# Scores of two heads from the two halves of the rows, weights scaled on GpSimd, and a new order, in a 512-token network kernel on one core

## The reference

```python
# first block, compressed/selected/window attention: 8 heads in 2 groups of 4, width 64, causal blocks of 128
ps = masked_softmax(jnp.einsum('bghqd,bgqmd->bghqm', qb, ksel) * scale, smask)
pw = masked_softmax(jnp.einsum('bghqd,bgkd->bghqk', qb, kwin) * scale, wmask)
on = gates[..., 0:1] * o_cmp + gates[..., 1:2] * o_slc + gates[..., 2:3] * o_win
# second block, even layer (differential attention, 4 heads, two softmax maps each)
sc = jnp.einsum('bqhmd,bshmd->bhmqs', qb, k).astype(f32) * scale
p = jax.nn.softmax(sc, axis=-1)
w = (p[:, :, 0] - lam * p[:, :, 1]).astype(v.dtype)
# second block, odd layer: 8 heads of width 96 (latent attention), then 8 heads in 2 groups, width 64
out_c = gqa_attention(q[:, :, :, None, :], k, v_c).reshape(b, s, MLA_HEADS * MLA_V)
out_d = gqa_attention(qd, kd, vd).reshape(b, s, GQA_Q_HEADS * GQA_DIM)
```

## Time and profile before

| | |
|---|---|
| median of 3 runs | 3011.55 us (3011.3 to 3012.63) |
| the profiled execution | 3006.02 us, of which the span from first to last instruction 3004.2 us |
| busy in the span | PE 2838.3 us (94%), PE weight loads 2327.3 (77%), DVE 1662.4 (55%), ACT 1139.8 (38%), POOL 205.2 (7%) |
| granted TensorE clock, mean | 0.976 of full |
| read from HBM | 238.31 MB, 80 GB/s over the span |

### The profile page before, as it was taken

The page is one execution under the profiler, slowest core; times in us unless marked ns, Lnnn a source line. Parts: engine busy times, 40 slices in busy tenths (PEclk is TensorE's granted clock), DMA queues, the critical chain, the costliest instruction groups (busy, mean ns, idle before and its releaser), DMA issues.

```text
span 3004.2 us, 33494 instructions
## 1 busy us (share of the span) xinstructions
PE 2838.3 (94%) x13102; PEld 2327.3 (77%) x13102; DVE 1662.4 (55%) x2501; ACT 1139.8 (38%) x1768; POOL 205.2 (7%) x194
## 2 busy tenths in 40 slices
PE   6997998999999999999799999999999887899999
PEld 5776776888878888877578888888887666688887
DVE  6467665555465443547854444544445987644433
ACT  4454563322233222344633222422233766432322
POOL 1001332000000000002100000000000321000000
PEclk9998999999999999999799999999999999999999
DMA  3212103332323333231023332333321110133322
GB/s 128 77 57 64 58 29 107 104 104 92 99 84 99 98 99 98 90 94 49 8 85 98 97 94 89 100 98 99 98 84 52 33 36 22 42 94 96 99 94 82
DMA packets 71181, 242.58 MB, mean 81 GB/s; under 512 B 8016, under 2 KB 9936, under 8 KB 70768
## 3 DMA queue, kind: packets, MB, share of 16 engines
q1 hardware_dynamic: 68112, 230.85, 24.5%
q0 software_dynamic: 1760, 7.49, 0.7%
q10 hardware_dynamic: 1152, 2.10, 0.2%
HBM read 238.31 MB, written 2.10 MB: 80 GB/s over the span
## 4 chain that ended last, share of the span: by engine, by line
PE 84%; DVE 11%; issue 2%; ACT 2%; POOL 0%; DMA 0%; DVEq 0%; ACTq 0%; POOLq 0%
PE ps L302 83%; DVE SC L325 3%; DVE SM L331 1%; PE ps L305 1%; DVE PTL L313 1%; DVE SC L313 1%; DVE WL L313 1%; DVE SC L319 1%; ACT SC L310 0%; DVE SC L328 0%; DVE NQ L313 0%; DVE SM L339 0%; DVE GQ L313 0%; POOL SC L313 0%; DMA PR<-par 0%
## 5 line engine op out<-in xcount | busy, mean ns | idle before, releaser
L302 PE MATMUL ps<-HH,WH 128*128 128x512 f32 (+1 forms) x2192 | 863.9, 394 | 15.2 <-DVE HL L325 13.6
L302 PE MATMUL ps<-HL,WH 128*128 128x512 f32 (+1 forms) x2192 | 856.4, 391 | 0.0
L302 PE MATMUL ps<-HH,WL 128*128 128x512 f32 (+1 forms) x2192 | 856.3, 391 | 0.0
L313 DVE TENSOR_TENSOR WL<-WF,WH 128x1024 fp32r<-128x1024 f32 (+3 forms) x473 | 546.6, 1161 | 355.8 <-ACT WH L310 353.0
L310 ACT ACTIVATE WH<-WF 128x1024 fp32r<-128x1024 f32 (+3 forms) x473 | 467.0, 993 | 645.3 <-PE ps L302 645.2
L302 PEld LDWEIGHTS ps<-HH,WH 128*128 128x128 f32 (+1 forms) x2192 | 413.5, 189 | 102.6 <-issue 15.3
L302 PEld LDWEIGHTS ps<-HH,WL 128*128 128x128 f32 (+1 forms) x2192 | 412.8, 188 | 88.3
L302 PEld LDWEIGHTS ps<-HL,WH 128*128 128x128 f32 (+1 forms) x2192 | 413.3, 189 | 84.3
L302 PE MATMUL ps<-AH,WH 128*128 128x512 f32 x880 | 342.7, 389 | 3.9 <-DVE AL L313 3.9
L302 PE MATMUL ps<-AH,WL 128*128 128x512 f32 x880 | 342.3, 389 | 0.0
L302 PE MATMUL ps<-AL,WH 128*128 128x512 f32 x880 | 342.3, 389 | 0.0
(11 more groups left out here) (292 smaller groups left out, 3081.2 us busy)
## 6 DMA issues: line engine op xcount, KB each, us to landing
WF<-wall SPq DMA_DIRECT2D x397, 512.0 KB, 3.5
WF<-wall SPq DMA_DIRECT2D x40, 384.0 KB, 2.9
WF<-wall SPq DMA_DIRECT2D x17, 256.0 KB, 2.6
X<-xT ACTq DMA_DIRECT2D x8, 256.0 KB, 11.8
X<-xT POOLq DMA_DIRECT2D x8, 256.0 KB, 2.9
outT<-X POOLq DMA_DIRECT2D x8, 256.0 KB, 2.3
WF<-wall SPq DMA_DIRECT2D x4, 288.0 KB, 3.0
LT<-late POOLq DMA_DIRECT2D x1, 1152.0 KB, 5.5
```

The lines of the kernel that those rows point to most:

```text
L302: return self.real.matmul(o, l, r, start=start, stop=stop, skip_group_check=True)
L313: return self.real.tensor_tensor(o, a, b, op) if self.real is not None else Uncounted()
```

## The change

**What it does.** (1) In N and G the two heads i and i+4, which use the two key groups, are scored together; in D the two softmax maps of a head. Query tiles now hold the high parts of both heads on their two halves of rows, a second tile the low parts, and the keys likewise. A pair takes six matmuls of 64 rows instead of four of 128, dealt out in turn to rows 0 to 63 and 64 to 127 and into two banks. (2) So a query or key tile pair is filled by one ACT copy and one POOL subtraction of 128x512 (`unstacked` holds everywhere but in Q), and no DVE work. (3) In D, L and G the scaling of the weights goes from DVE to POOL as a two-scalar `tensor_scalar`; in D the second scalar is lambda, which removes a small DVE product, and a new step `joined` holds the final subtraction. (4) N and G get a second set of `PT` tiles, so that a pair's two heads don't share one, and N a second product bank. (5) Arena places and the waits that guard them change, and with them the order tables of M, N, D, L and G. (6) `c_made` and `s_product` issue the same matmuls with the halves in alternation.

The tables (a line of each; the rest alters likewise) and the core of the diff:

```diff
-GATES_IN = {"M": (0, 23), "N": (0, 85)}
+GATES_IN = {"M": (0, 23), "N": (0, 72)}
 D_PLACE = {
-    "made": (0.265, -0.033), "largest": (0.768, 0), "raised": (1.266, 0.3), "normed": (2.206, 0.126),
+    "made": (0, 0.049), "largest": (0.863, -0.196), "raised": (1.686, -0.016), "normed": (2.107, 0),
+    "joined": (2.705, 0.048), "turned": (3.631, -0.082), "high": (3.752, 0.15), "low": (4.402, 0.011),
...
+def attend_pair(ph, pair, T, *ends):
+
+    core = ("largest", "raised", "normed", "turned", "high", "low")
+    steps = [("made", 0, (pair, T))]
+    for g, job in enumerate(heads_of(ph, pair)):
+        steps += [(s, g, (job, T)) for s in core] + ([(s, g, job) for s in ends[g]] if T == 3 else [])
+    return steps
...
     items = []
     for i in range(4):
-        for g in range(2):
-            a = [attend((i, g), T, PAIR + (("parts",) if g else ())) for T in range(4)]
-            items += a[:1] + ([rope(f"gq{i + 1}")] if g == 0 and i < 3 else []) + a[1:] + [[]]
+        for T in range(4):
+            items += [attend_pair("G", i, T, PAIR, PAIR + ("parts",)), []]
+            if T == 0 and i < 3:
+                items.append(rope(f"gq{i + 1}"))
+        items.append([])
     return in_turn(G_PLACE, *items)
...
+                if stage == "made" and ph in "NG":
+                    pair, T = key
+                    n, tk = 128 * (T + 1) if causal else S, slice(128 * T, 128 * T + 128)
+                    q, k, made = qk_of(ph, pair)
+                    heads = [(job, T) for job in heads_of(ph, pair)]
+                    for w in made + [w for head in heads for w in bank_left(ph, "s", head)]:
+                        e.wait_ge(*w)
+                    for i in range(3):
+                        for g, head in enumerate(heads):
+                            l, r = three([part[rows(g), tk] for part in q], [part[rows(g), 0:n] for part in k])[i]
+                            done = e.matmul(bank(ph, "s", head)[:, 0:n], l, r, i == 0, i == 2 and not causal)
...
                 elif stage == "made":
                     job, T = key
                     tk = slice(128 * T, 128 * T + 128)
-                    for w in q_made("D", f"eq{job}") + [pooled["D", "lo1", f"ek{job}"]]:
-                        e.wait_ge(*w)
+                    Q, K = EQ[job % 2], EK[job % 2]
+                    e.wait_ge(*pooled["D", "lo1", f"eq{job}"])
+                    e.wait_ge(*pooled["D", "lo1", f"ek{job}"])
                     for m in range(2):
-                        Q, K, p = EQ[job % 2][m], EK[job % 2][m], bank("D", f"s{m}", key)
                         for w in bank_left("D", f"s{m}", key):
                             e.wait_ge(*w)
-                        for i in range(2):
-                            done = e.matmul(p[:, :], Q[:, i, tk], K[:, :], i == 0, i == 1)
-                        done.then_inc(*scored("D", f"made{m}", key))
+                    for i in range(3):
+                        for m in range(2):
+                            l, r = three((Q[0][rows(m), tk], Q[1][rows(m), tk]), (K[0][rows(m), :], K[1][rows(m), :]))[i]
+                            done = e.matmul(bank("D", f"s{m}", key), l, r, i == 0, i == 2)
...
-                    if ph == "L" and key[0] == "m":
-                        e.activation(pair_of(ph, key)[0][:, :], y[0:96, :], ACT.Copy).then_inc(*split_high(ph, "hi1", key))
+                    if unstacked(ph, key):
+                        high, n = pair_of(ph, key)[0], rope_of(ph, key)[0]
+                        e.activation(high[:, :], y[0:n, :], ACT.Copy).then_inc(*split_high(ph, "hi1", key))
...
             for stage, key in order["D"]:
-                rope_stage("D", stage, key)
+                if stage == "normed":
+                    P, sm = tile("D", "P1", key), small("D", "m1", key)
+                    e.wait_ge(*stepped["D", "inverse1", key])
+                    e.wait_ge(*stepped["E", "lam"])
+                    e.wait_ge(*pooled.so_far())
+                    e.tensor_scalar(P, P, sm[:, 2:3], LM[:, 5:6], ALU.mult, ALU.mult).then_inc(*pooled("D", "normed", key))
+                else:
+                    rope_stage("D", stage, key)
...
+            for ph in "LG":
+                for stage, key in order[ph]:
+                    if stage == "normed":
+                        P, sm = tile(ph, "P", key), small(ph, "m", key)
+                        e.wait_ge(*stepped[ph, "normed", key])
+                        e.wait_ge(*pooled.so_far())
+                        e.tensor_scalar(P, P, sm[:, 2:3], cc("ones")[:, 0:1], ALU.mult, ALU.mult)\
+                         .then_inc(*pooled(ph, "normed", key))
...
-                    if ph != "N":
-                        e.wait_ge(*stepped[ph, "normed", key])
-                        e.tensor_scalar(P, P, sm[:, 2:3], None, ALU.mult).then_inc(*normed(ph, "normed", key))
...
-                    e.wait_ge(*stepped["D", "inverse1", key])
-                    e.wait_ge(*stepped["E", "lam"])
-                    e.tensor_tensor(sm1[:, 3:4], sm1[:, 2:3], LM[:, 5:6], ALU.mult).then_inc(*stepped("D", "lam", key))
-                    e.wait_ge(*stepped["D", "lam", key])
-                    e.tensor_scalar(P1, P1, sm1[:, 3:4], None, ALU.mult).then_inc(*stepped("D", "second", key))
                     e.reciprocal(sm0[:, 2:3], sm0[:, 1:2]).then_inc(*stepped("D", "inverse", key))
+                elif stage == "joined":
+                    P0 = tile("D", "P0", key)
                     e.wait_ge(*stepped["D", "inverse", key])
-                    e.scalar_tensor_tensor(P0, P0, sm0[:, 2:3], P1, ALU.mult, ALU.subtract).then_inc(*normed("D", "normed", key))
+                    e.wait_ge(*pooled["D", "normed", key])
+                    e.scalar_tensor_tensor(P0, P0, small("D", "m0", key)[:, 2:3], tile("D", "P1", key), ALU.mult, ALU.subtract)\
+                     .then_inc(*normed("D", "joined", key))
```

318 lines of the change are left out of this document (172 added, 146 removed).

## The result

The changed kernel takes 2966.02 us (median of 4 runs, 2962.81 to 2968.80) against 3011.62 before, a ratio of 0.9848 with a 95% interval of 0.9832 to 0.9864. The profiled execution took 2963.42 us, its span is 2961.6. The forecast of 2963 holds as a total, and the halves of the rows do work side by side. Its terms do not hold: D and L gave more than their upper bounds, G less than its lower one, N nothing. The total came out right by luck: the misses nearly cancel.

The account below looks back on a forecast made before the run. PE was taken to bound N, and DVE's work to hold PE up in D, L and G; 16 + 10 + 16 + 0 + 6 = 48 us off 3006.0 gives 2958, plus 5.5 for the median, 2963 us; range 2935 to 3000.

Parts of the forecast that it names:

- D, -23.8 for 16: Stage D: forecast gain of 16 us, near the lower end of 13.4 to 23, from work taken off DVE.
- the upper bound of 23: Stage D: at most 23 us saved, if PE were as full as in N (93.2 / 0.943 = 98.9 us).
- The rows foretold for it: Stage D: `EQ` and line-319 DVE rows gone, DVE below PE, clock above 0.83, joined subtraction perhaps next, with short waits.
- L, -18.1 for 10: Stage L: forecast gain of 10 us from taking the scaling, 28.1 us, off DVE.
- the 16.5: Stage L: upper bound of the gain, 16.5 us, all of PE's idle time; the lower bound was nothing.
- That POOL's rotary additions would not hurt: Stage L: an addition can wait 0.8 us for a scaling on POOL, but its reader is several items behind.
- the rival built on it (3036 us): D, L and G: POOL becomes the softmax's bottleneck and holds DVE up, 72 us at 0.9 per block; chance 0.06.
- G, -5.7 for 16: Stage G: forecast gain of 16 us, between 10.4 and 27, from scalings and query splits off DVE and more `PT` tiles.
- the lower bound of 10.4: Stage G: at least 10.4 us gained, the query split's 8.6% of the chain in 121 us.
- Scores, taken as 0: Scores by halves in N, D, G: zero taken, between gain by overlap and cost of entries; ends -12 and +33 us.
- The rival without overlap (2987 us): Scores in N, D, G: halves don't overlap, N pays 14 us, D and G about 10, gain 24; chance 0.18.
- N and its passage, +0.2 for -6: N: 4 of 10.8 us idle time go; passage before it: about 2 from the first query's split; together 6, between 0 and 12.

Follow-up runs that it names:

- before_scaling_on_pool: Kernel before, with GpSimd scaling the weights in two-scalar form in D, L and G, old order and lags kept: 3007.9 us, ratio 0.9991.
- scaling_on_vector: Changed kernel with the scaling of the weights back on VectorE in D, L and G: 2986.6 us, ratio 0.9917.
- same_half: Changed kernel with the score matmuls of both heads (N, G) and both maps (D) all read from rows 0 to 63: 3009.1 us, one run.
- three_gates_last: Changed kernel with the last three of N's 48 gate projection pieces moved to items 73, 75 and 77: 2955.95 us, ratio 0.9809.

## Why the prediction was right in its total and wrong in its terms

**D, -23.8 for 16, beyond the upper bound of 23.** Two steps failed. The price was made of work taken off DVE (24.9 us) and of chain shares, and the lags were left out of it; the runs show that the work is worth 3.4 us under the old lags and the lags 20 under the new work. And the upper bound divided PE's busy time, 93.2 us at a clock of 0.83, by N's fullness as if it stayed; the busy time holds the slow clock, and fell with it. The rows foretold for it are right: `EQ` and the scaling gone from DVE, DVE below PE, the clock above 0.83, the joined subtraction next, with few waits.

**L, -18.1 for 10, beyond the 16.5.** The same two. "All of PE's idle time" was no upper bound: PE's busy time fell by 7.6 us too, as the clock rose from 0.93 to 0.98. Measured, the wait for the scaling fell as described, from 16.0 (14.8 in the earlier trace rows) to 4.3. That POOL's rotary additions would not hurt is right: 1.410 us where they took 1.305.

The Trainium skill, GPSIMD Engine Reference, section Key points, has GpSimd and VectorE contend where a VectorE instruction takes two inputs from the on-chip memory (SBUF) or runs in a 2-port mode. The trace agrees that something is paid: in L the rotary products with both inputs there took 0.938 us, those that read PSUM 0.735. But with POOL busy 76 us for 51 before, the former took 0.938 us each for 1.003, and VectorE's copies of 128x384 0.672 for 0.573. VectorE's busy time without the scaling was 117.2 us for 118.1. So the contention did not become dearer in the sum, and the rival built on it (3036 us) did not come.

**G, -5.7 for 16, under the lower bound of 10.4.** The failed step is the reading of the chain: 8.6% for the query split were taken as a gain for sure. A chain names what ended last, not what comes next. In its place the traces show that nearly all of G's old waits went, 25.8 of 27.2 us, and 18.2 us of others came, while PE's busy time grew by 2.0 us as the clock of G fell from 0.91 to 0.86. Moved scaling alone gave 4.7 of the 5.7 (before_scaling_on_pool; 3.5 by scaling_on_vector), so the halves, the second pair of `PT` tiles, the new lags and the cheaper queries gave 1 to 2 together. Each of the two attempts to take a wait away there got another in its place. What would shorten G stays open.

**Scores, taken as 0.** The rival without overlap (2987 us) is refuted by same_half. Three steps are 0.69, the entry and exit about 0.21 (the earlier trace rows had 0.15 for the entry), and 0.90 is what the four stacked ones took. That holds for blocks of 512 columns, in D and G. In N the term failed, since it had no price for leaving the half rows. Counted from start to start in PE's timeline, without the idle time, the scores of N fell from 22.2 us before to 21.1 in three_gates_last (both with the clock at 1.00), but the 64 matmuls of the causal mask behind them rose from 4.9 to 9.2: 3.2 us more, 0.10 for each of the 32 groups. The Trainium skill, TensorE: Matmul & The Clock Gate, Part 3 (packing small matmuls), says that row groups run concurrently, and same_half agrees, 1.58 against 0.90. That alone saves nothing here, where the stacked matmuls of 128 rows took 0.91.

**N and its passage, +0.2 for -6.** The idle time did fall by 5.0 us. Against it stand two items of 4.5 us each. One is PE's work at full clock: PE is busy 178.9 us in three_gates_last and 174.5 before. The scores with their masks are 3.2 of it and the transposes behind them 2.5 (24.5 for 22.0); the rest gave 1.2 back. The other is the half clock at the end of N. I had written that N's idle time "can go"; it went from the middle and stayed at the end, where it costs the clock. Ahead of N the 3.8 us fit one `c_made`, which N's new table puts later, so that it falls into N: its 16 matmuls took 1.7 us there before, and PE waited 2.4 us for DVE ahead of them. That was not tried by itself. With the new N it began at 281.7 to 285.9 us in kernels that are alike up to there, with the old one at 285.5 to 290.0, so the size is not sure to some 4 us.

**The merge, +4.1, not foreseen.** It was taken as untouched. The traces show three parts. In the first 30 us the half clock lasts longer than before, 0.8 us. In the next 50 us PE waits once 3.1 us for DVE's `YL` where it waited 1.5, and the stretch is 1.6 us longer. And in E 1.6 us go by the clock alone, with the same order of matmuls and the same idle time (1.1 us in these stretches, where fewer matmuls get done after); before, and then after:

```profile
1297.40:1317.40 20.00, 18.90 (x92) 15.87 (x91) 7.00 (x10) 11.21 (x16) 0.00 (x0) 1.00 0.23 68
1300.10:1320.10 20.00, 18.90 (x85) 15.76 (x84) 7.00 (x10) 11.15 (x16) 0.00 (x0) 0.91 0.21 65
```

The longer wait and the clock of 0.91 recur in every kernel with the new N and in none of the three with the old one; why, was not tried. three_gates_last takes 1.5 us of the 4.1 away.

D and L together gave 16 more than forecast, G, N and the merge 21 less (10, 6 and 4). The total came out because these misses nearly cancel, and that is luck: no step of the prediction made them do so.

## What to carry to other kernels

Taking work off an engine and ordering the rest are one change: here either alone gave 3 to 8 us of D's 24. Before crediting a relieved engine, look what it does while others wait for it, and not how busy it is over the stage; with 72 of 107 us busy, the same 16 us of waits stood there, because other steps stood ahead in its queue. And read PE's busy time together with its clock. Here some short idle spells at a stage's end, 2.4 us together, were followed by a half clock that cost 6 us, and three pieces of work that could be done at any time were worth most just there.

## What the runs showed of the hardware

- Two groups of 64 rows work at once even where the three matmuls of one are issued before the three of the other: 0.90 us in both orders, 1.58 on one half. In another product alternation did matter. The small product of D (`s_product`) has other halves: all its matmuls read 128 rows, and they write two halves of 64 rows of the result. It has eight records for each half (16 in all), in succession before and alternated after:

```profile
1353.65 1.58 PE L302 MATMUL ps<-LP,VG 128*64 128x128 f32 x16
1355.16 0.50 PE L302 MATMUL ps<-HH,WH 128*128 128x512 f32 x1
```

```profile
1365.83 1.09 PE L301 MATMUL ps<-LP,VG 128*64 128x128 f32 x16
1366.85 1.12 PE L301 MATMUL ps<-SC,C 128*128 128x512 f32 x2
```

  It takes 1.51 us to the next operation before and 1.02 after, at a clock of 1.00 in both. Before, the second half's first record starts 0.49 us after the first half's, beside its fifth, and after it starts with it. Whether the number of matmuls in a row or the kind of halves makes the difference from the scores wasn't tried.
- Full-row matmuls behind a group on half rows are dearer: 64 mask matmuls in N took 4.9 us behind stacked scores and 9.2 behind the groups of six.
- After the idle spells of 457 to 462 us the clock stood at 1.2 GHz for 12 us of nearly unbroken matmuls; with 18 matmuls put between, it stayed at 2.4 GHz, though a wait of 0.4 us remained.
- The same D, with nearly the same waits, ran 3 us apart at a clock of 0.86 or 0.92, and the same N 1.7 us apart with 1.00 or 0.66 in its first 10 us.
